# Norm's root, mixing's order and GpSimd's share of the low parts in an encoder trunk

## What is computed

```
x += 1/2 * gate1 * SwiGLU_1(adaLN(RMSNorm(x)))
x += gate2 * W_out( sig(g_a) * W_ao(SWA-GQA-sinks(u)) + sig(g_p) * W_po(MultiPool(u)) ),  u = adaLN(RMSNorm(x))
x += 1/2 * gate3 * SwiGLU_2(adaLN(RMSNorm(x)))
```

## Time and profile before

| | before |
|---|---|
| median of three runs | 1985.67 us |
| lowest, highest | 1985.27, 1988.31 us |
| the profiled execution: time, span | 1982.75, 1981.0 us |
| instructions | 31974 |
| ScalarE, GpSimd busy | 852.1, 175.4 us |
| mean granted clock of TensorE | 0.997 |
| read from memory | 261.07 MB, 133 GB/s |

### The profile page before, as it was taken

How to read it: one execution, slowest core, us unless ns; L and a number is a source line. 1 busy time by engine, 2 the same in 40 slices (tenths; PEclk the granted TensorE clock), 3 DMA queues, 4 the chain that set the end, 5 groups by cost and what they waited for, 6 DMA issues and landing times.

```text
span 1981.0 us, 31974 instructions
## 1 busy us (share of the span) xinstructions
PE 1948.7 (98%) x12475; PEld 1748.7 (88%) x12475; DVE 1481.8 (75%) x2298; ACT 852.1 (43%) x1495; POOL 175.4 (9%) x115
## 2 busy tenths in 40 slices
PE   9999999999999999999999999999999999999999
PEld 7889989887788889999998999998777888999998
DVE  5887897786777868878787887877766878668572
ACT  3434535333522545445453534444343235445351
POOL 1000021301000000020300002030200000000202
PEclk9999999999999999999999999999999999999999
DMA  9655353534445243544434454344444433334332
GB/s 297 195 157 158 108 161 112 137 116 163 139 131 166 78 147 106 173 144 121 152 116 139 116 161 149 108 150 91 160 131 154 141 96 85 108 91 122 97 102 80
DMA packets 343812, 265.23 MB, mean 134 GB/s; under 512 B 49246, under 2 KB 325922, under 8 KB 343664
## 3 DMA queue, kind: packets, MB, share of 16 engines
q1 hardware_dynamic: 342960, 262.63, 44.6%
q0 software_dynamic: 400, 0.38, 0.1%
q10 hardware_dynamic: 304, 0.19, 0.0%
HBM read 261.07 MB, written 2.10 MB: 133 GB/s over the span
## 4 chain that ended last, share of the span: by engine, by line
PE 86%; DVE 5%; ACT 2%; issue 2%; DMA 2%; SPq 1%; ACTq 0%; DVEq 0%
PE bank L2382 11%; PE bank L2384 11%; PE bank L2383 11%; PE bank L2223 10%; PE bank L2225 10%; PE bank L2224 10%; PE ps L2223 4%; PE ps L2224 4%; PE ps L2225 4%; PE bank L2307 2%; PE bank L2308 1%; PE bank L2311 1%; DVE ada_acc L1566 1%; PE ps L2384 1%; PE ps L2383 1%
## 5 line engine op out<-in xcount | busy, mean ns | idle before, releaser
L2382 PE MATMUL bank<-u_hi,w_hi 128*128 128x256 f32 x1120 | 317.4, 283 | 7.5 <-issue 4.4
L2383 PE MATMUL bank<-u_lo,w_hi 128*128 128x256 f32 x1120 | 317.2, 283 | 0.0
L1013 ACT ACTIVATE w_hi<-stage 128x1024 fp32r<-128x1024 f32 (+3 forms) x259 | 219.8, 867 | 175.0 <-DMA stage<-in_w_pool_o 48.9
L936 POOL TENSOR_TENSOR w_lo<-stage,w_hi 128x640 fp32r<-128x640 f32 (+2 forms) x71 | 146.8, 2080 | 1596.7 <-ACT w_hi L1013 1558.0
L2223 PE MATMUL bank<-u_hi,w_hi 128*128 128x512 f32 x648 | 258.7, 399 | 0.4 <-DVE prod L1669 0.4
L2225 PE MATMUL bank<-u_hi,w_lo 128*128 128x512 f32 x648 | 252.5, 390 | 0.0
L2224 PE MATMUL bank<-u_lo,w_hi 128*128 128x512 f32 x648 | 252.4, 390 | 0.0
L2384 PE MATMUL bank<-u_hi,w_lo 128*128 128x256 f32 x840 | 238.0, 283 | 0.0
L1406 DVE TENSOR_TENSOR w_lo<-stage,w_hi 128x1024 fp32r<-128x1024 f32 (+2 forms) x189 | 186.8, 994 | 51.4 <-ACT w_hi L1013 50.3
L2382 PEld LDWEIGHTS bank<-u_hi,w_hi 128*128 128x128 f32 x1120 | 215.0, 192 | 10.1 <-issue 5.2
L2383 PEld LDWEIGHTS bank<-u_lo,w_hi 128*128 128x128 f32 x1120 | 215.0, 192 | 0.9
(11 more groups left out here) (291 smaller groups left out, 4362.1 us busy)
## 6 DMA issues: line engine op xcount, KB each, us to landing
stage<-in_w_ff_up SPq DMA_DIRECT2D x172, 512.0 KB
ada_stage<-in_w_ada SPq DMA_DIRECT2D x80, 512.0 KB, 4.6
ada_stage_mix<-in_w_ada SPq DMA_DIRECT2D x48, 512.0 KB, 4.6
stage<-in_w_ff_down SPq DMA_DIRECT2D x24, 960.0 KB
stage<-in_w_in SPq DMA_DIRECT2D x16, 1024.0 KB
stage<-in_w_ff_down SPq DMA_DIRECT2D x16, 896.0 KB
ada_block<-in_w_ada SPq DMA_DIRECT2D x8, 1024.0 KB, 11.9
stage<-in_w_out SPq DMA_DIRECT2D x8, 1024.0 KB
```

What stands on the lines that cost most here:

```text
L936: nc.gpsimd.tensor_tensor(raw_tile(w_lo, e, key), raw_tile(stage, e, key), hi_tile(e, key), ALU.subtract).then_inc(lo_ready, 1)
L1013: nc.scalar.activation(hi_tile(e, key), raw_tile(stage, e, key), ACT.Copy).then_inc(hi_ready, 1)
L2382: mm(dst, hi[:, k, :], r_hi_[:, k, :], start=(k == 0 and w in (1, 7)), stop=False, skip_group_check=True)
L2383: mm(dst, hi[:, k, :], r_lo_[:, k, :], start=False, stop=False, skip_group_check=True)
```

## The change

1. **The root.** At the end of an FF event ScalarE does the root for h = 0 ahead of rounding the next event's third first tile, where it did it after; at the end of mixing likewise. TensorE's `first_tiles` asks for two tiles at its start and for the third only when its turn comes at h = 0, k = 0. VectorE adds the last squares of the second half one step later, behind a low part of u.
2. **Pooling.** `pool_mix(l, 3)` stands at the end of the tile n = 10, ahead of the low part and the ada piece there; it stood at the start of n = 11.
3. **The first vector in mixing.** Its transposes and reductions move from behind n = 13 to behind n = 14 (`turn_first`), where no piece is taken; the pieces behind it come one tile later, the last at n = 44.
4. **Out tiles.** For n = 42 to 47 the low part of the tile n + 3 comes after the update of x and the addition of squares, and not before.
5. **Low parts.** VectorE makes those of p = 0 alone, GpSimd those of p = 1, 2 and 3: 8 instructions in each of the four FF events, 32 in all, change the engine. In event 0 one ada piece moves from `("D", 0, 3)` to `("D", 1, 0)`.

```diff
@@ -210,6 +210,9 @@
 ALL_PIECES = [(v, k) for group in ADA_SETS for v in group for k in range(KT)]
+T_TURN = 14
+
+
 def piece_points(e):
@@ -220,9 +223,9 @@
         return [(RUN_ENDS[p], 0)] * count
     if e % 3 == 1:
-        return [("M", n) for n in (*range(6, 26), 42, 42, 43, 43)]
+        return [("M", n) for n in (*range(6, T_TURN), *range(T_TURN + 1, 26), 42, 42, 43, 43, 44)]
     if e == 0:
-        return ([("U", n) for n in (7, 7, 8, 8, 9, 9, 10, 10)] + down(0, 1, 2, 3, 3) + last_of(1, 3) + down(1, 1, 2, 3)
+        return ([("U", n) for n in (7, 7, 8, 8, 9, 9, 10, 10)] + down(0, 1, 2, 3) + last_of(1, 3) + down(1, 0, 1, 2, 3)
                 + last_of(2, 3) + down(2, 0, 1, 2) + last_of(3, 2) + down(3, 0, 1, 1, 2, 2, 3))
     if e in (2, 3):
         return (last_of(0, 2) + down(0, 0, 1, 2) + last_of(1, 3) + down(1, 1, 2, 3) + last_of(2, 3) + down(2, 0, 1)
@@ -938,8 +941,8 @@
             def last_down(e):
-                pool.wait_ge(lo_ready, lo_done(e, ("D", PARTS - 3, KT - 1)))
-                for p in (PARTS - 2, PARTS - 1):
+                pool.wait_ge(lo_ready, lo_done(e, ("D", 0, KT - 1)))
+                for p in range(1, PARTS):
                     for m in range(KT):
                         low_part(e, ("D", p, m))
                 if e + 1 < STAGES:
@@ -1057,6 +1060,7 @@
                     square(e, m)
                 else:
                     root(*divmod(e, 3), 0)
+                    round_weights(e, first_tile(e, AHEAD - 1))
                     square(e, KT)
             def round_u(l, i):
@@ -1203,7 +1207,7 @@
                     elif not final:
                         for step in (("A1", "A22"), ("S1", "S23"), ("S4",))[m + AHEAD - KT]:
                             round_block(e, end + 1, step)
-                    elif after:
+                    elif after and m < KT - 1:
                         round_weights(e + 1, first_tile(e + 1, m + AHEAD - KT))
                     if m == 1 and not final:
                         if end >= first_pair(e):
@@ -1254,7 +1258,7 @@
                 for n in range(MIX_TILES):
                     if n == MIX_TILES - 1:
                         square(event(l, 1) + 1, KT - 1)
-                    if not T_P <= n < T_Y:
+                    if not T_P <= n < T_Y and n < MIX_TILES - 1:
                         ahead(e, n + AHEAD)
                     if n == T_P + 1:
                         for h in range(2):
@@ -1494,12 +1498,11 @@
                 dve.wait_ge(vec_step, vec_before(l, i) + 2)
                 for q in range(U_STEPS):
                     scaled(q)
-                    if last_update and q == 1:
-                        add_squares(event(l, i), KT - 1)
                     if q:
                         low(q - 1)
                     if last_update:
                         if q == 2:
+                            add_squares(event(l, i), KT - 1)
                             last_update()
                         if 4 <= q < 7:
                             for step in ((0,), (1, 2), (3, 4))[q - 4]:
@@ -1565,7 +1568,7 @@
                     dve.wait_ge(ada_used, count)
                     nc.vector.scalar_tensor_tensor(ada_acc[:, :], src, c_k, ada_acc[:, :], ALU.mult, ALU.add
                                                    ).then_inc(ada_used, 1)
-                if k == KT - 1:
+                if k == KT - 1 and (e % 3 != 1 or a != KT - 1):
                     n, group = next((n, group) for n, group in enumerate(ADA_SETS) if v in group)
                     sum_group(v, group.index(v), n)
                     if v == group[-1]:
@@ -1606,6 +1609,11 @@
                     ins = nc.vector.tensor_reduce(ada_sum[q * SQ:(q + 1) * SQ, at:at + len(group) * KT], quads[:, q, :, :],
                                                   AX_X, ALU.add)
                 ins.then_inc(ada_added, 1)
+
+            def turn_first(e):
+
+                n, group = next((n, group) for n, group in enumerate(ADA_SETS) if PIECES[e][0][0] in group)
+                sum_group(group[0], 0, n)
             def pieces(e, point):
                 for a, taken in enumerate(POINTS[e]):
@@ -1815,7 +1823,7 @@
                     low_blocks(e, j + 1, "S1", "A22", "S4")
                 elif again:
                     low_h(e, j - 1)
-                if last and p < PARTS - 2:
+                if last and p == 0:
                     low_part(e, ("D", p, 0))
                     low_part(e, ("D", p, 1))
                 pieces(e, (j, 0))
@@ -1833,7 +1841,7 @@
                 for m in range(KT):
                     if ahead and m == KT - 2:
                         low_part(e + 1, first_tile(e + 1, 1))
-                    if p < PARTS - 2 and m + 2 < KT:
+                    if p == 0 and m + 2 < KT:
                         low_part(e, ("D", p, m + 2))
                     if m == 1 and end < first_pair(e):
                         low_t4(e)
@@ -2019,9 +2027,9 @@
                 dve.wait_ge(lo_ready, LO_BASE[e] + AHEAD)
                 for n in range(MIX_TILES):
-                    if not T_V <= n < T_OUT and n < MIX_TILES - 2:
+                    if n < T_V:
                         low_ahead(e, n + AHEAD)
-                    if T_P + 2 <= n <= T_P + 5:
+                    if T_P + 2 <= n <= T_P + 4:
                         pool_mix(l, n - T_P - 2)
                     if n == T_P + 3:
                         norm_k(l)
@@ -2055,10 +2063,13 @@
                         update_x(e, n, n - T_OUT, bank[n % BANKS])
                     elif n == MIX_TILES - 2:
                         close_first(l, 1)
-                        low_ahead(e, n + AHEAD)
-                    if T_V <= n < T_OUT:
+                    if n == T_P + 4:
+                        pool_mix(l, 3)
+                    if T_V <= n < MIX_TILES - 1:
                         low_ahead(e, n + AHEAD)
                     pieces(e, ("M", n))
+                    if n == T_TURN:
+                        turn_first(e)
             def angle_step(step):
@@ -2294,8 +2305,8 @@
                 e = event(l, i)
                 pe.wait_ge(x_updated, x_before(l, i) - 2)
-                pe.wait_ge(hi_ready, HI_BASE[e] + FIRST)
-                pe.wait_ge(lo_ready, LO_BASE[e] + FIRST)
+                pe.wait_ge(hi_ready, HI_BASE[e] + FIRST - 1)
+                pe.wait_ge(lo_ready, LO_BASE[e] + FIRST - 1)
                 for h in range(2):
                     frames = slice(h * FH, (h + 1) * FH)
                     for k in range(KT):
@@ -2304,7 +2315,12 @@
                         pe.wait_ge(u_hi_ready, step)
                         for n in range(FIRST):
                             hi, lo = hi_tile(e, first_tile(e, n)), raw_tile(w_lo, e, first_tile(e, n))
+                            third = h == 0 and k == 0 and n == FIRST - 1
+                            if third:
+                                pe.wait_ge(hi_ready, HI_BASE[e] + FIRST)
                             mm(bank[n][:, frames], hi[:, k, :], u_hi[:, k, frames], start=(k == 0), stop=False)
+                            if third:
+                                pe.wait_ge(lo_ready, LO_BASE[e] + FIRST)
                             mm(bank[n][:, frames], lo[:, k, :], u_hi[:, k, frames], start=False, stop=False)
                         pe.wait_ge(u_lo_ready, step)
                         for n in range(FIRST):
```

## The result

The changed kernel takes 1963.56 us, the median of three runs (1962.0 to 1965.31), against 1985.67 before: 0.9885 of it, 95% interval 0.9863 to 0.9908. The forecast was 1972.8 (1965 to 1981): the sign was right, the time outside the range. The profiled executions are 1982.75 and 1963.56, spans 1981.0 and 1961.7, so 19.2 apart in the trace; the forecast's own sum was 12.9. Run again beside experiments, on one chip, the changed kernel had 1965.46 and the one before 1985.11 (0.9901, 0.9886 to 0.9916), 19.7 apart. The 2.4 by which the first 22.1 is more lie within the spread of the runs.

The account below looks back on a forecast made before the run. TensorE, busy 98% of the span, was taken as the bound, leaving some 32 us. Terms 6.5 + 1.8 + 3.0 + 2.1 + 2.4 - 2.7 - 0.2 = 12.9 less gave a median of 1972.8, range 1965 to 1981.

Parts of the forecast that it names:

- The signs it named: Waits for y under 0.5, pooling and squares gone, softmax under 0.6, squaring 0.16, clock near 1.00 behind event 0's end.
- "Issue": TensorE's two waits in event 0 behind the first and second parts, 4.4 before; forecast about 5.6, the second near 3.0.
- Root, 6.5: Norm's root ahead of the third tile's rounding, so GpSimd no longer holds VectorE's squaring: all five y waits go, 6.5 won.
- The clock, 1.8: Behind the two y waits over 2.2 the granted clock no longer falls: 0.9 won at each, 1.8.
- Pooling 3.0: Fourth pooling group's mixing comes 2.3 sooner, more than TensorE's wait of 1.5: 3.0 won for two layers.
- the first vector 2.1: First vector's sums in mixing one tile later free the attention softmax: 2.6 less 0.25 left per layer, 2.1 won.
- squares 2.4: Out tiles of mixing, low part last: x and squares no longer wait behind ScalarE's rounding, all 2.4 won.
- GpSimd makes the low parts of the second part: Event 0's second-part wait grows by 1.2 to 3.0, and the clock's fall costs 1.5: 2.7 lost.
- the upper bound: Event 0, GpSimd holding nothing: 0.8 to 1.8 gained, as a low part of 0.8 also leaves VectorE before the first block's.
- The other three events, -0.2: First low part at most 0.5 later, inside TensorE's 0.9 of slack: 0, with 0.2 lost for all three.
- the prediction's own bound of 19.7: All bounds favourable, clock 3.4, attention 2.6, event 0 plus 1.8: 19.7 less, 1966; 1 more for the unseen sets the lower end.
- The third rival: GpSimd's second-part low parts hold VectorE 2.03 instead of 0.82 each, 9.7 an event: 2006, half holding 1988; chance 0.07.

Follow-up runs that it names:

- experiments 1 and 4: On the kernel before: 1, the norm's part alone, 0.9961 of before; 4, only the root ahead of the third tile's rounding, third tile still awaited, 0.9967.
- the ladder: Changed kernel with 6, 9, 12, 15 and 18 extra roots ahead of the norm's root at the five borders between events; 0.9961 of before.
- experiment 3: Kernel before with GpSimd making the second part's low parts and the one ada piece moved, nothing else; 1.0002 of before.
- experiments 2 and 3: On the kernel before: 2, the pooling, first-vector and out-tile parts alone, 0.993 of before; 3, GpSimd's low parts and moved ada piece alone, 1.0002.
- the one reordering of the queue tried here: Changed kernel with every ada load of event 0 one load later in SyncE's queue, 0.9906 of before; second part's low parts back on VectorE, 0.9911.

## Why the prediction missed

- **The signs it named:** y's, the pooling's and the squares' waits gone, the squaring at 0.16 each, the clock at 1.00 behind the first event's end: as said. "Issue" came at 3.3 where 5.6 was said, and event 0's second wait at 1.59 where about 3.0 was said.
- **Root, 6.5:** right in mechanism, and the listed 6.5 went whole; experiments 1 and 4. The five waits and the 2.18 of the squaring went together.
- **The clock, 1.8:** 2.2 (1.39 + 1.32, less 0.26 each), right in kind and in the right two places; the working took the middle of 0 and 1.7. That a wait over 2.2 brings the fall is not borne out (2.47, 2.68 and 2.79 brought none in other kernels), so it is in part luck that the term fits.
- **Pooling 3.0 and the first vector 2.1, squares 2.4:** the listed waits went whole, 3.0, 2.6 and 2.4. The 0.5 held back for the next attention step was not needed; TensorE waits nowhere in it.
- **A step that failed, at 2.65: "6.5", "3.0", "2.4" as the price of waits.** The sum took the bracket of a row for the whole cost. Each of the waits had 0.26 beside it (0.25 to 0.3 in the changed kernel, 0.15 + 0.10 step by step in the ladder), save the softmax with 0.08: 2.65 in all.
- **The step that failed most, at 2.7 of its own and 0.2 for the other events: "GpSimd makes the low parts of the second part", the wait of event 0 from 1.79 to 3.0.** It was 1.59 in the changed trace and 1.86 in experiment 3, whose whole trace is 0.2 longer. The first half of that working was right: angle steps held, the issue 1.55 late where 1.2 was taken. It left out that the load would then take 0.8 less, and it counted the 0.8 of the low part that goes only in the upper bound. It also had the clock fall for certain there. It fell at this place in experiments 2 and 3 and in one of the two profiled executions of the changed kernel, at 1.6 a time; that it did not in the first is luck.
- **The other three events, -0.2:** 0.0.
- **The reference:** 19.2 is the trace's difference and 22.1 the medians'. The trace's difference lies inside the prediction's own bound of 19.7; the rest is spread, for which the lower end had room for 1 only, in a kernel whose clock falls or not at several waits. The second set's 19.7 apart would have been 1966.0.

By the numbers: 12.9 + 2.65 (the 0.26s) + 2.9 (GpSimd) + 0.5 (softmax) + 0.4 (clock) = 19.35, against the 19.3 of the table. The third rival, VectorE held so long that the time gets worse, did not occur: of the 9.7 it took per event, the sums in events 2, 3 and 5 had one held instruction of 1.95, as predicted. The rule of the Trainium skill (SBUF - State Buffer, "SBUF: two separate sides") that the prediction cites for two inputs in SBUF has a second case, a VectorE instruction in a 2-port performance mode. The angle step of line 2081 has one tensor input and was held as well (1.68 for 0.49 before), so the first case does not cover it; whether the second does, no row here tells.

## What to carry to other kernels

Price a wait of TensorE by the difference in start times across it, not by the bracket of its row: here 0.26 more at nine waits and 0.08 at two, nearly a fifth of what they list. Before counting a helper engine's slowing of another, follow the delay on to the transfer it holds up and the instruction it frees: of 1.55 late nothing was left where TensorE waited. And look at what a slot's release hangs on: cutting a load into 2, 3, 3 in place of 3, 3, 2 gave 4 us that the one reordering of the queue tried here did not give.

## What the runs showed of the hardware

Whether the clock falls behind a wait isn't set by the wait's length. It fell behind 1.04, 1.74, 1.86, 1.95, 2.06, 2.17, 2.38 and 3.32, among others, and stayed up behind 1.89, 1.98, 2.08, 2.20, 2.47, 2.68, 2.79 and 3.14, and behind most waits of 1.0 to 1.8. At one and the same place, ahead of the pair behind event 0's first part, it fell behind 2.66 and 3.32 and stayed up behind 2.68 and 3.14. A fall cost 1.5 to 1.7 where TensorE was the bound (6 us at 0.72), 1.0 to 1.1 at the borders. Once, in the ladder's kernel behind event 0's first part (a wait of 3.16), it stayed down longer: 0.53 over 124 to 130, where the changed kernel has 0.74, and 0.9 more was lost. What decides it stays open; the matmuls and their order are the same in all these kernels. It explains a good part of the 2 to 9 us by which executions of one kernel differ: the granted clock that the runs report goes from 1.0 to 0.997 as the changed kernel's time goes from 1962.0 to 1965.31, and from 0.998 to 0.994 as that of the kernel before goes from 1980.85 to 1989.78.
